# Six split slots, a mask made on TensorE, offsets spread through longer rows and a separate turn of q in a two-layer hybrid encoder

## The reference

```python
for l in range(DEPTH):                                   # 2
    h = _rms(x, norm_g[l])
    p = jnp.einsum('bsd,de->bse', h, w_in[l])            # 256x1024 by 1024x11808
    ...
    y_a = _mixer_deltanet(...)       # 4 heads, chunks of 64: a triangular solve, then a scan, both directions
    y_b = _mixer_natten(...)         # 8 heads, neighbourhood attention on the 4x64 grid
    y_c = _mixer_gqa(...)            # 4 heads, full attention with rotary positions
    y_d = _mixer_mlstm(...)          # 4 heads, a chunked scan, both directions
    proj = jnp.einsum('bsnw,nwd->bsnd', ys, w_branch[l])
    gates = jax.nn.sigmoid(gate_logits.reshape(B, S, N_BRANCH, D_MODEL))
    x = x + jnp.einsum('bsd,de->bse', jnp.sum(gates * proj, axis=2), w_out[l])
```

```python
bias = rpb[:, row_off[:, None, :, None], col_off[None, :, None, :]]
s = jnp.where(in_win[:, None, :], s + bias[None].astype(F32), -jnp.inf)
```

## Time and profile before

| | us |
|---|---|
| median of 3 runs (1095.15 to 1103.41) | 1102.85 |
| the profiled execution | 1100.24 |
| its span, first to last instruction | 1098.4 |
| TensorE busy, matmuls | 932.9 |
| VectorE busy | 689.9 |
| ScalarE busy | 539.0 |
| GpSimd busy | 263.1 |

### The profile page before, as it was taken

The page is one execution under the profiler, slowest core; times in us unless marked ns, Lnnn a source line. Parts: engine busy times, 40 slices in busy tenths (PEclk is TensorE's granted clock), DMA queues, the critical chain, the costliest instruction groups (busy, mean ns, idle before and its releaser), DMA issues. The chain is left out here.

```text
span 1098.4 us, 19683 instructions
## 1 busy us (share of the span) xinstructions
PE 932.9 (85%) x7190; PEld 768.2 (70%) x7190; DVE 689.9 (63%) x1145; ACT 539.0 (49%) x1050; POOL 263.1 (24%) x268
## 2 busy tenths in 40 slices
PE   4888789889888898989858888798898889989896
PEld 3887568667766777767657876686776657767775
DVE  3876774546368666575558767654563696665763
ACT  3775445444344654545347754444443345554552
POOL 1452210322424003210024511112323240131100
PEclk9989989999999998999968999999899998999999
DMA  7544655325264343446255446464253633344553
GB/s 192 152 132 117 144 119 126 93 66 148 69 161 127 97 134 115 128 143 209 96 124 164 118 109 147 108 128 115 59 137 82 167 115 91 122 119 150 162 189 110
DMA packets 106669, 139.69 MB, mean 127 GB/s; under 512 B 30910, under 2 KB 51654, under 8 KB 106438
## 3 DMA queue, kind: packets, MB, share of 16 engines
q1 hardware_dynamic: 99382, 137.34, 45.9%
q10 hardware_dynamic: 7184, 1.02, 0.6%
HBM read 135.17 MB, written 6.82 MB: 129 GB/s over the span
## 5 line engine op out<-in xcount | busy, mean ns | idle before, releaser
L1457 DVE TENSOR_TENSOR w_low<-ring,w_high 128x512 fp32r<-128x512 f32 x464 | 342.9, 761 | 246.5 <-ACT w_high L1128 245.9
L1128 ACT ACTIVATE w_high<-ring 128x512 fp32r<-128x512 f32 x464 | 287.3, 630 | 316.1 <-PE pj L646 204.2
L644 PE MATMUL pj<-w_high,h_high 128*128 128x512 f32 x592 | 249.3, 421 | 42.1 <-DVE w_low L1457 23.0
L645 PE MATMUL pj<-w_low,h_high 128*128 128x512 f32 x592 | 240.2, 406 | 0.0
L646 PE MATMUL pj<-w_high,h_low 128*128 128x512 f32 x592 | 239.8, 405 | 0.0
L644 PEld LDWEIGHTS pj<-w_high,h_high 128*128 128x128 f32 x592 | 117.3, 198 | 75.9 <-DVE w_low L1457 38.4
L646 PEld LDWEIGHTS pj<-w_high,h_low 128*128 128x128 f32 x592 | 116.8, 197 | 26.5
L645 PEld LDWEIGHTS pj<-w_low,h_high 128*128 128x128 f32 x592 | 117.2, 198 | 23.6
L1133 ACT ACTIVATE big<-pair 128x512 f32<-128x512 f32 (+2 forms) x136 | 60.1, 480 | 21.7 <-PE pair L638 7.1
L2079 POOL TENSOR_TENSOR zbuf<-zbuf,mid 128x512 f32<-128x512 f32 x20 | 26.3, 1338 | 133.3 <-DVE mid L1883 133.3
L1978 POOL TENSOR_TENSOR big<-big,tab 128x256 f32<-128x256 f32 x40 | 33.2, 849 | 91.8 <-PE pair L821 59.8
(11 more groups left out here) (284 smaller groups left out, 1681.3 us busy)
## 6 DMA issues: line engine op xcount, KB each, us to landing
ring<-in_w_in SPq DMA_DIRECT2D x368, 256.0 KB, 3.0
ring<-in_w_branch SPq DMA_DIRECT2D x64, 256.0 KB, 3.1
ring<-in_w_out SPq DMA_DIRECT2D x32, 256.0 KB, 2.7
big<-skew SPq DMA_DIRECT2D x32, 128.0 KB, 3.9
skew<-in_na_rpb SPq DMA_DIRECT2D x16, 224.0 KB
out_x<-btm SPq DMA_DIRECT2D x12, 256.0 KB, 3.9
btm<-out_x SPq DMA_DIRECT2D x8, 256.0 KB, 4.9
tab<-in_table SPq DMA_DIRECT2D x1, 1408.0 KB, 7.6
```

What stands on the lines that cost most here:

```text
L644: mm(o, r32(a), r32(b), start=start, stop=False, skip_group_check=True)
L645: mm(o, r32(a), r32(b_low), start=False, stop=False, skip_group_check=True)
L1128: f(r32(w_high[:, u % PARTS]), ring[:, u % RAW], ACT.Copy).then_inc(w_rounded, 1)
L1457: tt(r32(w_low[:, u % PARTS]), ring[:, u % RAW], w_high[:, u % PARTS], ALU.subtract).then_inc(w_split, 1)
```

## The change

Four edits are made together.

1. `ring`, `w_high` and `w_low` get six places (RAW, PARTS = 6). The splits stay four units ahead in the sequence (LEAD = 4). The plan is now kept by unit instead of by block part, and `branch` is a `proj` step like the others; its merge on VectorE and GpSimd stands at the same place. To make room in SBUF, several tensors of the solve and of mixer d share their places in another way (`num` now lies over `bias`, `mqT` over `nqT`).
2. The offsets go in two moves: `repeat_rpb` copies each head's 7 rows, 8 times each, to a small HBM tensor `lines`, one head every second unit from the third `conv` block on; `spread_rpb` copies each of the 7 runs of 8 rows (4 KB) 8 times from `lines` to `skew`, where the spread stood before. The first of them waits for all of `lines`.
3. `b_window` is gone. VectorE rounds the identity and the window to fp32r at the end of `b_prep`; in `b_score` TensorE first writes identity times window, repeated over the bank, and then adds the scores to it.
4. The turn of `q_dec` and its copy are a step `qd` of their own, which stands once behind `("uw", 1)` for chunk 0 and behind `scan_v` for chunk 1, and for chunks 2 and 3 behind `("uw", 3)`.

The `load_bias` DMAs stand two units later in the queue, since their place is counted from RAW.

```diff
-WB, UN = 512, 4
-RAW, PARTS = 4, 4
+WB, CUN = 512, 4
+RAW, PARTS, LEAD = 6, 6, 4
+SIZES = (4, 4)
...
-        ("uw", 0), 1, ("uw", 1), ("scan_v", 0), ("scan_o", 0))
+        ("uw", 0), 1, ("uw", 1), ("qd", 0), ("scan_v", 0), ("qd", 1), ("scan_o", 0))
...
-    add(("uw", 2), ("scan_v", 2), ("uw", 3), ("scan_o", 2), 1, ("scan_v", 3),
-        ("scan_o", 3), ("a_sum",), 1, ("b_window",), ("a_gate", 0), ("a_gate", 1), 1, ("a_out", 0), ("a_out", 1), 2)
+    add(("uw", 2), ("scan_v", 2), ("uw", 3), ("qd", 2), ("qd", 3), ("scan_o", 2), 1, ("scan_v", 3),
+        ("scan_o", 3), ("a_sum",), 1, ("a_gate", 0), ("a_gate", 1), 1, ("a_out", 0), ("a_out", 1), 2)
...
-                if split and name in ("proj", "branch"):
-                    n = block_no[(args[0], args[1])] if name == "proj" else block_no[("branch", tuple(args))]
-                    due = range(UN * n + PARTS, min(UN * (n + 1) + PARTS, UN * len(plan)))
-                    steps[name](*args, due)
+                if split and name == "proj":
+                    kind, arg, u, n = args
+                    unit = unit_no[(kind, arg, u)] + LEAD
+                    steps[name](*args, range(unit, min(unit + n, len(plan))))
...
+                    def qd(s):
+                        j, b = s % 2, sd[s % 2]
                         pe.wait_ge(scaled_uw, 4 * s + 3)
                         pe.wait_ge(*room(b, ("qd", s)))
                         turn4(b, [q_dec[:, j, h] for h in range(H)])
...
                     def b_score(t, q):
                         pe.wait_ge(*released(("nqk", 1, 1)))
+                        pe.wait_ge(window_rounded, 2)
                         for par in range(2):
                             pe.wait_ge(*room(mb[par], ("bs", t, q, par)))
+                            o = mb[par].t.rearrange("p (k c) -> p k c", c=GRID)
+                            mm(o, r32(eye_r), r32(over(window_r, 2 * STEPS)), start=True, stop=False, skip_group_check=True)
...
+                    def repeat_rpb(h):
 
                         table = na_rpb[layer, h]
                         first = table.offset + 4 * RPB_C + WIN - 1 - (GRID - 1)
-                        src = bass.AP(table.tensor, first, [[RPB_C, 7], [0, C], [1, P]])
-                        sp.dma_start(skew[h], src).then_inc(rpb_spread, 16)
+                        src = bass.AP(table.tensor, first, [[RPB_C, 7], [0, REP], [1, P]])
+                        sp.dma_start(lines[h], src).then_inc(rpb_lines, 16)
+
+                    def spread_rpb(h):
+
+                        if h == 0:
+                            sp.wait_ge(rpb_lines, 16 * NAH)
+                        src = bass.AP(lines.tensor, h * 7 * REP * P, [[REP * P, 7], [0, C // REP], [1, REP * P]])
+                        dst = bass.AP(skew.tensor, h * 7 * C * P, [[C * P, 7], [REP * P, C // REP], [1, REP * P]])
+                        sp.dma_start(dst, src).then_inc(rpb_spread, 16)
...
-                        first = block_no[("c", (1, 1))]
-                        if unit % UN == 0 and 0 <= unit // UN - first < NAH:
-                            spread_rpb(unit // UN - first)
-                        after = unit - (UN * block_no[("o", (0, 1))] + RAW)
+                        repeat, spread = unit - unit_no[("conv", 2, 0)], unit - unit_no[("c", 1, 4)]
+                        if repeat % 2 == 0 and 0 <= repeat // 2 < NAH:
+                            repeat_rpb(repeat // 2)
+                        if spread % 4 == 0 and 0 <= spread // 4 < NAH:
+                            spread_rpb(spread // 4)
+                        after = unit - (unit_no[("o", 0, 4)] + RAW)
                         if 0 <= after < 2 * NT * STEPS:
                             load_bias(after)
...
+                        ts(r32(eye_r), ident, 1.0, None, ALU.mult).then_inc(window_rounded, 1)
+                        ts(r32(window_r), K("window"), 1.0, None, ALU.mult).then_inc(window_rounded, 1)
...
-                    def b_window():
-                        for t in range(NT):
-                            pool.wait_ge(bias_in[t], 16 * 2 * STEPS)
-                            v = bias[:, t].rearrange("p h (k c) -> p (h k) c", k=STEPS)
-                            pool.tensor_tensor(v, v, over(K("window"), NAH * STEPS), ALU.add).then_inc(windowed, 1)
```

More of the change, by code:

```diff
@@ L211, in weight_plan, with depth @@
     for name, *args in stages:
[L212 to L219, removed]
-            plan.append((args[0], args[1], first[args[0]] + WB * args[1][0]))
-    return plan
+        if name != "proj":
+            continue
+        kind, arg, u, n = args
+        if kind == "branch":
+            col = arg[1] * WB
+        elif kind == "gate":
+            col = GATES + arg[0] * D + arg[1] * WB
+        else:
+            col = first[kind] + arg * (CW if kind == "conv" else WB)
+        plan += [(kind, arg, u + i, col) for i in range(n)]
+    return plan
+def depth(kind):
+    return {"conv": CUN, "branch": BK}.get(kind, KT)
 def build(nc, x_in, norm_g, w_in, conv_a, dn_a_log, dn_dt_bias, dn_norm_g, na_q_norm, na_k_norm, na_rpb,
@@ L700, in product @@
                         def product(t, u):
-                            if k0 + u == 0:
+                            if u == 0:
                                 pe.wait_ge(*room(banks[t], ("pj", kind, block, t)))
-                            w = [v[:, (UN * n + u) % PARTS] for v in (w_high, w_low)]
-                            h = [v[:, k0 + u, t * P:(t + 1) * P] for v in tokens]
-                            last = split_product(banks[t].t, h, w, k0 + u == 0, k0 + u == depth - 1)
+                            unit = unit_no[(kind, block, u)]
@@ L706, in product @@
+                            if t == 0:
+                                pe.wait_ge(w_split, unit + 1)
+                            w = [v[:, unit % PARTS] for v in (w_high, w_low)]
+                            h = [v[:, u, t * P:(t + 1) * P] for v in tokens]
+                            last = split_product(banks[t].t, h, w, u == 0, u == deep - 1)
                             if t == NT - 1:
                                 last.then_inc(weights_used, 1)
-                            elif k0 + u == depth - 1:
+                            elif u == deep - 1:
@@ L724, in proj @@
-                    def proj(kind, arg):
+                        u = u0
+                        while u < u0 + count:
+                            n = 2 if u in (0, deep - 2) and u + 2 <= u0 + count else 1
+                            for t in range(NT):
+                                for v in range(u, u + n):
+                                    product(t, v)
+                            u += n
+                    def proj(kind, arg, u, n):
                         if kind == "conv":
-                            conv_product(arg)
+                            conv_product(arg, u, n)
@@ L727, in proj @@
                             return
[L728 to L731 removed]
+                        if kind == "out" and arg == 0 and u % 4 == 0:
+                            pe.wait_ge(*released(("mT", 1, u // 4)))
+                        if kind == "branch" and u == 0:
+                            pe.wait_ge(y_split, BRANCHES.index(arg[0]) + 1)
@@ L1060, in load_unit @@
                     def load_unit(unit):
[L1062 to L1063 removed]
+                        kind, arg, u, col = plan[unit]
                         if unit >= RAW:
@@ L1208, in proj @@
+                            if kind == "conv" and u0 + count == depth(kind):
+                                conv_take(arg)
+                            return
+                        for u in due[:-2]:
                             split(u)
-                        act.wait_ge(*front(kind, block))
-                        evict(kind, block, 0)
-                        for u in due[2:3]:
+                        act.wait_ge(*front(kind, arg))
+                        evict(kind, arg, 0)
+                        for u in due[-2:-1]:
@@ L1681, in residual, with proj @@
                         tt(v, v, b.t, ALU.add).then_inc(b.free, 1)
-                    def proj(kind, arg, due):
-                        if kind == "conv" or arg[1] == 0 or (kind[0] != "z" and kind != "out"):
+                    def proj(kind, arg, u0, count, due):
+                        last = u0 + count == depth(kind)
+                        if kind == "branch":
+                            for u in due:
+                                split(u)
+                            if last:
+                                merge(arg)
+                            return
+                        if not last or (kind[0] != "z" and kind != "out"):
                             for u in due:
```

198 lines of the change are left out of this document (88 added, 110 removed).

## The result

The changed kernel takes 1046.66 us in the median (1044.77 to 1048.24), the kernel before on the same chip 1102.4 us: a ratio of 0.951, interval 0.948 to 0.954. The gain is 55.7 us; I had forecast 32.2 us, to 1070, with a range that ended at 1052. The direction was right, the size was not.

A forecast was written before the change was run, and what follows sets the result against it. TensorE's own work plus about 165 us idle was taken as the bound. Terms 10.8 + 5.4 + 7.0 + 2 + 7 = 32.2 us from 1100.24 gave 1068.0, adjusted to the median 1070 us; range 1052 to 1092.

The forecast's parts named there:

- Six split slots: ScalarE's splits wait for a later TensorE release, so evictions and scan copies start earlier: 2 us, between 0 and 8.
- The lines: Offsets' spread in 4 KB rows, priced with the deeper raw ring: weight loads behind it land sooner, 10.8 us gained.
- my third of the waits for L1978 and L1349: Waits in the spread's stretch with partly the same cause; a third of their 12.6 us, 4.2 us, was to go.
- The turns: Reordered turns of `q_dec` behind `uw`: fewer TensorE waits for ScalarE's bank, 7.0 us gained, between 3 and 10.
- the 0.6 us for GpSimd's scaling: Allowance in the turns' price: GpSimd's scaling for the second pair's next `uw` ends last, 0.3 us per layer.
- The mask: TensorE product replaces GpSimd's window addition: 9.1 us of stalls removed, 3.7 us of products added, net 5.4 us gained.
- The clock: TensorE's half-clock stretches behind the removed waits return to full clock: 7 us gained, between 0 and 14.
- the first term: Offsets' spread and six-unit raw ring together: waits for L1230 gone, other waits in that stretch shorter, 10.8 us.
- That the spread gets no faster: Rival: 4 KB HBM-to-HBM rows hold loads behind them as long as 512 B rows; about 1082 us, chance 0.17.
- That other engines take the place of what is removed: Rival: in solve and attention, VectorE and GpSimd waits replace those removed, half the sum arrives; 1086 us, chance 0.15.
- The slower case: Rival: mask products lengthen each score group's chain and stalls move to other GpSimd instructions; about 1108 us, chance 0.05.
- Loads behind a spread land in 3 to 4 us: Sign in the new profile: weight loads queued behind the offsets' spread from `lines` land in 3 to 4 us.

The follow-up runs named there:

- e3: The changed kernel with raw ring and split slots both set back to four: 1068.5 us.
- e2: The changed kernel with the raw ring set back to four, split slots still six: 1051.5 us.
- e1: The changed kernel with split slots set back to four, raw ring still six: 1068.2 us.
- e9: The changed kernel unaltered, measured again in a later session: 1047.44 us, ratio 0.949 to the kernel before.
- e13: The changed kernel with both rings at four and lines, mask product and turn order all taken back: ratio 0.996 to the kernel before.
- e10: The changed kernel with raw ring four, six split slots, and lines, mask product and turn order taken back: 1080.7 us, ratio 0.979 to the kernel before.
- e16: The changed kernel with both rings at four, keeping only the eightfold lines: 10.5 us less than with those taken back too (e13).
- e14: The changed kernel with both rings at four, keeping only the mask as a product: 12.6 us less than with that taken back too (e13).
- e6: The changed kernel with GpSimd adding the window again, both rings at six: 1 to 4 us slower than the changed kernel.
- e5: The changed kernel with both rings at four and the old spread, keeping mask product and turn order: about 22 us less than e13.
- e4: The changed kernel with the old spread of 512-byte rows and no lines, both rings at six: 1 to 4 us slower than the changed kernel.
- e8: The changed kernel keeping only both rings at six, with old spread, GpSimd's window and old turn order: 1054.3 us.
- e7: The changed kernel with each turn of `q_dec` straight behind its `uw` again, both rings at six: 1049.2 us.

## Why the prediction was right or wrong

**The failed step: "Six split slots".** I wrote of the 204.2 us that "nothing is TensorE's idle time by itself" and took "2 us, between 0 and 8". The slots give 17 to 21 us at every setting that I tried (e3 to e2, e1 to e9, e13 to e10). The sentence is true as far as it goes; what I left out is what stands behind its wait in program order. I priced one split at the end of a block, 0.6 us, as if that happened a few times. It happens at many hand-overs between ScalarE, VectorE and TensorE: the gate merge (L1908), the merge before `w_out` (L1921), mixer `d`'s scaled scores (L1870), `c`'s exponentials (L1367), and I had looked only at the long single waits. Of the 11 and 7 us of the late stretches, where I had no term, some 6 in each go back with four slots (e1). Of the other 5 us of the first layer the slots are not the cause: e13, which has none of the parts, is already 6.8 us shorter than the kernel before in this stretch, with 3.4 us at half clock in it against 17.1. So it is mostly clock; whether the rewriting or chance brought it is not shown.

**The three other parts**, at the depth of before, came near their prices, two of them by other terms than mine. The lines gave 10.5 to 10.8 us against 10.8. From e13 to e16 the waits for L1239 go as I said (7.8 us), but nothing of my third of the waits for L1978 and L1349 does: the first grow from 3.8 to 8.1 us, the second stay. Other waits shrink instead, one for VectorE (L1623, 4.5 to 0.7 us) and one for ScalarE (L1147, 3.8 to 1.1). Idle time falls by 13.0 us, and the busy time rises by 5.3 with more half clock. The turns gave 6.9 us against 7.0. The four waits of 0.69 us are left as I had named them, and nothing shows of the 0.6 us for GpSimd's scaling; but `scan_v` now waits 2.4 us, for which I had no term, so idle time falls by 4.9 us only. That the time fell by 6.9 all the same is clock or scatter: luck.

The mask gave 8 to 13 us against 5.4 net. Between the same products in e13 and e14 the two stretches with its three stalls are 5.0 us shorter in the first layer and 4.6 in the second, 9.6 us with the added products paid, where I had 9.1 before them and 5.4 after. Idle time falls by 12.5 us in all, and the busy time rises by 4.3, about the added products; so it is not clock that was given back. Two things were missing in my term. The scores waited 5.2 us for the bank that VectorE frees, and the mask's products now wait 3.2 there: part of their own time falls into a wait that was there. And GpSimd's second add held a VectorE instruction as well:

```profile
334.12 5.27 DVE L1715 TENSOR_TENSOR y_low<-big,y_high 128x1024 fp32r<-128x1024 f32 x1 [0.25 <-ACT y_high L1227]
```

It takes 1.23 us in e14, as its like elsewhere do. In e6, with six slots, the first add falls on yet another one (L1672, 5.1 us against 0.7).

**The clock** was 7 us in my sum; from e13 to e3 the busy time fell by 8.5 us (928.2 to 919.7) with 3.7 us of products added, so it was some 12 us. As the sum of all terms but the slots' was 30.2 us and e3 is 36 us below the kernel before by its ratio, of which the rewriting has 4, this miss is small.

**The sum.** I added five terms as if they were independent. The three small ones are at the depth of four, and shrink to 1 to 4 us each once the rings are deep. The raw ring had no price of its own in it, only a share in the first term: it is worth nothing at four slots (e1 against e3), 2 to 5 us with six slots and the three parts, and 26 us with six slots without them. A cover's price depends on what else covers the same lateness.

**The rivals.** That the spread gets no faster (0.17) is ruled out: e3 and e5 differ by it alone, 10.8 us (1.0% by their ratios, whose intervals do not touch), and the loads behind it land in 4 us. The rule cited there, of the Trainium skill, "DMA: Bandwidth & Descriptors", section Specifications, that 512 B reach line rate, would have given nothing; at that depth the measurement decides against it here, and at the full depth (e4) its worth can't be seen. That other engines take the place of what is removed (0.15) did not decide: in the changed kernel the waits that I had named as its sign shrank, for L1978 (L2003 after) from 6.6 to 4.2 us and for L1349 (L1367) from 6.0 to 3.5. In single steps it did happen, with the lines alone (3.8 to 8.1 us) and at `scan_v` (2.4 us). The slower case (0.05) did not come: the wait at the score bank is 3.3 us (L965), none over 0.9, against 5.2 before.

**The signs named.** Loads behind a spread land in 3 to 4 us: nearly, 3.6 to 5.3. ScalarE's waits for `ring` under 25 us: 9.4. No VectorE split near the end of the scan over 1.5 us: the splits of the changed kernel, by duration in ns (least, median, longest), have none over 1.78 us, where the earlier trace rows showed 4.67:

```profile
L1475 DVE TENSOR_TENSOR w_low<-ring,w_high x464: 675/684/1784, 18.5 to 1027.5; 128x512 fp32r<-128x512 f32 x155
```

Half-clock stretches fewer: 16 instead of 20, and the two of the earlier trace rows are gone. TensorE's idle time down by some 25 us: 39, the 14 beyond it are about what the slots give (12 to 16).

**What stays open.** How the slots' gain divides over the hand-overs: I can name rows for 12 to 16 us of idle time; the rest is busy time, part of it clock that differs from run to run. What in the rewriting gives the 4 us of e13. Whether a placement of another kind (splits put behind the hand-over steps, with four slots) would give the same without the memory was not tried. No version ran below the changed kernel.

## What to carry to other kernels

A wait on an engine with time to spare is free only if nothing behind it in that engine's program order is waited for: before calling it slack, look at what stands next in line at each hand-over, and count the hand-overs. A ring as deep as the distance at which it is filled has no slack, and one slot more may give nearly all of it (five of six slots gave 18 of 21 us here). Price a cover together with the others on the same stall: alone at depth four the lines gave 10.5 us, at full depth some 2.

## What was unexpected of the hardware

Small differences in TensorE's waits go with its granted clock: at one place of each layer, 1.83 us of idle time was followed at once by a stretch at 0.50 in seven of sixteen cases, and 1.57 us in none of twenty. Over the whole program the time at half clock ran from 71 to 116 us in the traces and followed the medians only loosely (e8 71.1 us at 1054.3, e3 78.5 at 1068.5, e7 88.5 at 1049.2), and the kernel before and e13, 4 us apart, had 112.8 and 102.0. Half of a difference in half clock is lost, so by these two I put the error of a clock term from one profile at some 5 us, an estimate.

A DRAM-to-DRAM spread of 224 KB in 448 rows of 512 bytes let the load behind it land after 7.5 to 9.1 us, the same bytes in 56 rows of 4 KB after 3.6 to 5.3; on the time it was worth 10.8 us where nothing covered it and none that could be measured where a deeper ring did.
